# The modulation vector's products on VectorE inside the feed-forward stage, in a transformer block with a mixture of experts

## What is computed

```python
def first_block(...):
    h = h + fox_mixer(rms_norm(h, attn_norm), ...)
    gate, up = jnp.split(rms_norm(h, ffn_norm) @ ffn_w_in, 2, axis=-1)
    h = h + (jax.nn.silu(gate) * up) @ ffn_w_out
    return rms_norm(h, final_norm)
# the second block: c is (1, 1024), w_ada (1024, 6144)
mod = jax.nn.silu(c) @ w_ada + b_ada      # six vectors of 1024: shift, scale and gate, twice
```

## Time and profile before

| | |
|---|---|
| median of 3 runs | 2544.54 us |
| span of the profiled execution | 2545.1 us |
| TensorE busy | 2352.3 us, 92% |
| VectorE, ScalarE, GpSimd busy | 907.3, 738.5, 766.2 us |
| DMA | 597.33 MB, mean 235 GB/s |
| first feed-forward tile to end of the stage | 442.9 to about 811 us |

### The profile page before, as it was taken

The page is one execution under the profiler, slowest core; times in us unless marked ns, Lnnn a source line. Parts: engine busy times, 40 slices in busy tenths (PEclk is TensorE's granted clock), DMA queues, the critical chain, the costliest instruction groups (busy, mean ns, idle before and its releaser), DMA issues.

```text
span 2545.1 us, 26948 instructions
## 1 busy us (share of the span) xinstructions
PE 2352.3 (92%) x11046; PEld 1448.3 (57%) x11046; DVE 907.3 (36%) x1584; ACT 738.5 (29%) x1181; POOL 766.2 (30%) x488
## 2 busy tenths in 40 slices
PE   8999999999999999999999997998888888888885
PEld 5677557788888788787777883332322222322221
DVE  2634552100004799846775334211111111111113
ACT  3434562322223323348676222100100000001001
POOL 3233643454554344344233624110000100000000
PEclk9999999999999999999999998999999999999997
DMA  4344313532323333333335347999999999999994
GB/s 167 114 155 155 102 40 133 165 116 86 104 75 100 102 99 82 124 138 116 133 116 197 139 182 305 421 426 426 426 426 426 426 426 425 426 424 423 423 424 196
DMA packets 174202, 597.33 MB, mean 235 GB/s; under 512 B 18243, under 2 KB 97091, under 8 KB 148352
## 3 DMA queue, kind: packets, MB, share of 16 engines
q1 hardware_dynamic: 154992, 562.23, 56.8%
q10 hardware_dynamic: 8416, 23.92, 2.4%
q0 software_dynamic: 10672, 9.46, 1.1%
HBM read 591.02 MB, written 28.97 MB: 244 GB/s over the span
## 4 chain that ended last, share of the span: by engine, by line
PE 57%; DMA 24%; DVE 12%; ACT 4%; issue 2%; SPq 0%; POOL 0%; ACTq 0%; DVEq 0%; POOLq 0%
DMA arena<-in_w 14%; PE ps L785 11%; PE ps L787 10%; PE ps L786 10%; DMA ring<-in_w 9%; PE ps L1332 8%; DVE ps L2238 5%; PE ps L1330 3%; PE ps L1351 3%; DMA ring<-in_w_in 1%; PE ps L867 1%; ACT arena L1434 1%; PE ps L812 1%; PE ps L836 1%; PE ps L985 1%
## 5 line engine op out<-in xcount | busy, mean ns | idle before, releaser
L2684 POOL TENSOR_TENSOR ring_r<-ring,ring_r 128x1024 fp32r<-128x1024 f32 x220 | 511.6, 2332 | 687.3 <-ACT ring_r L1423 687.2
L785 PE MATMUL ps<-r,ring_r 128*128 128x512 f32 (+1 forms) x1536 | 611.9, 398 | 1.4 <-DVE arena L2226 1.2
L787 PE MATMUL ps<-r,ring_r 128*128 128x512 f32 (+1 forms) x1536 | 599.6, 390 | 0.0
L786 PE MATMUL ps<-r,ring_r 128*128 128x512 f32 (+1 forms) x1536 | 599.2, 390 | 0.0
L1434 ACT ACTIVATE arena<-ps 128x512 f32<-128x512 f32 (+4 forms) x274 | 183.2, 686 | 1145.5 <-PE ps L1332 854.1
L1332 PE MATMUL ps<-arena 128*64 128x512 f32 x672 | 325.5, 641 | 62.5 <-DMA arena<-in_w 62.1
L1330 PE MATMUL ps<-arena 128*64 128x512 f32 x688 | 345.6, 651 | 3.1 <-issue 3.0
L785 PEld LDWEIGHTS ps<-r,ring_r 128*128 128x128 f32 (+1 forms) x1536 | 287.6, 187 | 78.2 <-issue 14.6
L786 PEld LDWEIGHTS ps<-r,ring_r 128*128 128x128 f32 (+1 forms) x1536 | 287.8, 187 | 64.2 <-issue 4.3
L787 PEld LDWEIGHTS ps<-r,ring_r 128*128 128x128 f32 (+1 forms) x1536 | 287.4, 187 | 63.2
L1423 ACT ACTIVATE ring_r<-ring 128x1024 fp32r<-128x1024 f32 x220 | 222.9, 1015 | 322.2 <-PE ps L787 217.5
(11 more groups left out here) (357 smaller groups left out, 2466.4 us busy)
## 6 DMA issues: line engine op xcount, KB each, us to landing
arena<-in_w SPq DMA_DIRECT2D x106, 2048.0 KB, 39.1
ring<-in_w SPq DMA_DIRECT2D x86, 2048.0 KB, 37.5
ring<-in_w_ada SPq DMA_DIRECT2D x12, 2048.0 KB
ring<-in_ffn_w_in SPq DMA_DIRECT2D x22, 1024.0 KB
ring<-in_w_in SPq DMA_DIRECT2D x40, 512.0 KB
ring<-in_w_in SPq DMA_DIRECT2D x8, 2048.0 KB
ring<-in_fox_w_in SPq DMA_DIRECT2D x7, 2048.0 KB
arena<-acs_d SPq DMA_DIRECT2D x16, 512.0 KB, 3.5
```

Of the source, the lines that this page charges most:

```text
L785: e.matmul(out, wh[:, k, :], X.hi[:, k0 + k, :], start=first and k == 0, stop=False)
L786: e.matmul(out, wh[:, k, :], X.lo[:, k0 + k, :], start=False, stop=False)
L787: m = e.matmul(out, wl[:, k, :], X.hi[:, k0 + k, :], start=False, stop=last and k == nk - 1)
L2684: e.tensor_tensor(GL[t], grans[t][1], GH[t].bitcast(F32), ALU.subtract).then_inc(sem["gr_lo"], 1)
```

## The change

All twelve modulation tiles are made inside the feed-forward stage. VectorE multiplies and accumulates the eight blocks of a tile in two accumulators `AD` and adds them into `ADS`, which raises the semaphore `adv`; TensorE only sums `ADS` over the partitions, by `ones`. TensorE's products, ScalarE's copies and their places in the PSUM bank table are gone. The loads stand between the weight loads of the feed-forward stage, tile 0 to 5 with the pairs of tiles of the first half, 6 to 9 with the four blocks of the first down projection, 10 and 11 with the first two pairs of the second half. `order` exchanges every modulation load but the first with the load ahead of it. The slot of a modulation load is released by `adv`. The first rows of c go to the other slot, and their places in SyncE's list are renumbered.

```diff
+def ada_after(nt):
+    return (nt // 2 + 4 * (nt > 11),) if nt % 2 == 1 and 0 < nt < 16 else ()
+def ada_between(half, nt):
+    return (6 + nt // 2,) if half == 0 and nt % 2 == 1 else ()
 ...
     for k0, n in HALVES:
         for nt in range(k0, k0 + n, 2):
             two(a["ffn_w_in"], 128 * nt, FH + 128 * nt)
-            if nt < 8:
-                ada(8 + nt // 2)
+            for i in ada_after(nt + 1):
+                ada(i)
         for c in range(4):
 ...
+            for i in ada_between(k0 // 12, 2 * c + 1):
+                ada(i)
 ...
-        NCK0 = cols(RG[:, 0:1824], 2)
+        NCK0 = cols(RG[:, WC:WC + 1824], 2)
+        AD, ADS = [A[:, 26752 + 512 * i:27264 + 512 * i] for i in range(2)], A[:, 27776:28288]
 ...
-            return [(ps("ada", n).full, ps("ada", n).n + 1)]
+            return [(sem["adv"], n + 1)]
 ...
-            def ada(n):
 ...
-                    m = e.matmul(u.ap[32 * g:32 * g + 32], SC[:, k:k + 1].broadcast_to([128, 32]), aw[:, k, :], start=k < 4, stop=k >= 4)
+            def ada_columns(n):
+                u = ps("adb", n)
+                w.wait_ge(sem["adv"], n + 1)
                 w.wait_ge(u.free, u.n)
+                for j in range(4):
+                    m = e.matmul(u.ap[:, j:j + 1], ADS[:, j * 128:(j + 1) * 128], ones[:, 0:1], start=True, stop=True)
                 m.then_inc(u.full, 1)
 ...
                         whole("hu", nt, X=XF)
-                    if nt in (1, 3, 5):
-                        ada(9 + nt // 2)
+                    for n in ada_after(nt):
+                        ada_columns(n)
 ...
                             tile(u.ap, XH[half], u, k0=r, first=r == 0, last=r == 8)
+                        for n in ada_between(half, 2 * c + j):
+                            ada_columns(n)
 ...
+            def ada(n):
+                i, aw = ada_load[n]
+                w.wait_ge(sem["sc"], 1)
+                w.wait_ge(loads[i].slot, loads[i].value)
+                for k in range(8):
+                    acc = AD[k % 2]
+                    if k < 2:
+                        e.tensor_scalar(acc, aw[:, k, :], SC[:, k:k + 1], None, ALU.mult).then_inc(d.next(), 1)
+                    else:
+                        two_back()
+                        e.scalar_tensor_tensor(acc, aw[:, k, :], SC[:, k:k + 1], acc, ALU.mult, ALU.add).then_inc(d.next(), 1)
+                last()
+                e.tensor_tensor(ADS, AD[0], AD[1], ALU.add).then_inc(sem["adv"], 1)
 ...
                     e.tensor_tensor(x, x, u.ap, ALU.mult).then_inc(u.free, 1)
-                    if nt in (2, 4, 6):
-                        mod(8 + nt // 2)
+                    for n in (9,) if nt == 12 else ada_after(nt - 1):
+                        mod(n)
+                    for n in ada_after(nt + 1):
+                        ada(n)
 ...
                     e.tensor_tensor(hT[:, nt, NM:L], hT[:, nt, NM:L], u.ap, ALU.add).then_inc(u.free, 1)
+                    for n in (5,) if (half, nt) == (0, 0) else ada_between(half, nt - 1):
+                        mod(n)
+                    for n in ada_between(half, nt + 1):
+                        ada(n)
 ...
             order = list(range(len(loads)))
             for n, (i, _) in ada_load.items():
-                if n in (5, 6) or n >= 8:
+                if n > 0:
                     order[i - 1], order[i] = i, i - 1
```

More of the change, by code:

```diff
@@ L59 @@
         "nsq", "nrm", "lp_d", "lp_a", "cscan", "nckm", "qk", "sdone", "pmax", "pexp", "prec", "pnorm", "pv", "o_hi", "o_lo",
-        "fn", "fn_hi", "hid_hi", "hid_lo", "x2", "n1", "n1_hi", "uzero", "cv", "xbc", "bc", "alog", "acs",
+        "fn", "fn_hi", "adv", "hid_hi", "hid_lo", "x2", "n1", "n1_hi", "uzero", "cv", "xbc", "bc", "alog", "acs",
         "tk_d", "tk2", "cvc", "cvn", "cv_s", "cv_hi", "xs", "cb", "mrel", "mexp", "mm", "xd", "yg", "yl",
@@ L146, in bank_table @@
     t = ps.take
[L148 to L151, removed]
     def norm(stage, j, skip=()):
@@ L171, in bank_table @@
         t("ks", c)
-        ada(c, True)
     t("f", 0)
@@ L217, in bank_table @@
             t("hg", nt)
-            if nt in (2, 4, 6):
-                t("adb", 8 + nt // 2)
             t("hu", nt)
-            if nt in (1, 3, 5):
-                ada(9 + nt // 2)
+            for n in ada_after(nt):
+                t("adb", n)
         for nt in range(8):
             t("fo", half, nt)
+            for n in ada_between(half, nt):
+                t("adb", n)
     t("fin")
@@ L857, in spread @@
                 e.matmul(u.ap, ones, RST[:, :T], start=True, stop=True).then_inc(u.full, 1)
-            def ada(n):
[L860 to L863, removed]
+            def ada_columns(n):
+                u = ps("adb", n)
+                w.wait_ge(sem["adv"], n + 1)
                 w.wait_ge(u.free, u.n)
-                for k in range(8):
-                    g = k % 4
-                    m = e.matmul(u.ap[32 * g:32 * g + 32], SC[:, k:k + 1].broadcast_to([128, 32]), aw[:, k, :], start=k < 4, stop=k >= 4)
+                for j in range(4):
+                    m = e.matmul(u.ap[:, j:j + 1], ADS[:, j * 128:(j + 1) * 128], ones[:, 0:1], start=True, stop=True)
                 m.then_inc(u.full, 1)
[L870 to L876, removed]
             def meta(u, ld, raw):
@@ L1056, in pe @@
                         whole("hg", nt, X=XF)
-                        if nt in (2, 4, 6):
-                            ada_columns(8 + nt // 2)
                         whole("hu", nt, X=XF)
-                    if nt in (1, 3, 5):
-                        ada(9 + nt // 2)
+                    for n in ada_after(nt):
+                        ada_columns(n)
                 for c in range(4):
@@ L1973, in head_norm, with two_back @@
                 e.scalar_tensor_tensor(x, x, gain, RST[:, :n], ALU.mult, ALU.mult).then_inc(sem["nrm"], 1)
+            def two_back():
+                w.wait_ge(d.sem, d.n - 1)
+            def ada(n):
[11 more added lines that the diff above has]
+                e.tensor_tensor(ADS, AD[0], AD[1], ALU.add).then_inc(sem["adv"], 1)
             def mod(n):
@@ L2047, in dve @@
                 e.tensor_copy(kT[:, 4 * c:4 * c + 4, 0:NM], cols(u.ap[:, 0:64], 4)).then_inc(u.free, 1)
-                mod(c)
             for i in range(2):
@@ L2065, in dve @@
                 e.tensor_copy(vm[:, c * 512:(c + 1) * 512], u.ap[0:16]).then_inc(u.free, 1)
-                mod(2 + c)
             for nt in range(8):
-                if nt == 4:
-                    mod(4)
                 head_norm("q", nt)
-            mod(5)
             for nt in range(2):
                 head_norm("g", nt)
-            mod(6)
             w.wait_ge(sem["nrm"], 16)
@@ L2112, in dve @@
                 e.tensor_tensor(hT[:, nt, NM:L], hT[:, nt, NM:L], u.ap, ALU.add).then_inc(u.free, 1)
-                if nt in (4, 6):
-                    mod(7 + nt // 6)
                 if nt >= 3:
@@ L2862, in sp @@
                         w.wait_ge(s, value)
-                if i == 16:
+                if i == 9:
                     w.wait_ge(sem["c_d"], 16)
@@ L2872, in sp @@
                     e.dma_start(dst, src).then_inc(ld.slot, 16)
-                if i == 9:
+                if i == 5:
                     w.wait_ge(sem["cscan"], 1)
                     e.dma_start(a["c_d"], cT).then_inc(sem["c_d"], 16)
-                if i == 16:
+                if i == 9:
                     for p in range(2, 8):
```

52 lines of the change are left out of this document (removed).

## The result

The changed kernel takes 2688.3 us (median of four runs, 2687.07 to 2695.58) against 2544.17 us for the kernel before on the same chip: 1.0565 times as long, 95% interval 1.055 to 1.058. On another chip the ratio was 1.0575 (1.0556 to 1.0593). The profiled execution, one of the two quickest of the four, spans 2685.3 us, 140.2 us more than that of before; its mean granted clock is 0.937.

The account below looks back on a forecast made before the run. TensorE was taken to bound the kernel, busy for 92% of 2545.1 us. From 2544.5 us, -28.3 + 1.6 + 159.9 + 27, less 0.84, gave +159.4 and 2704 us, with 2668 to 2742 for 8 in 10.

Parts of the forecast that it names:

- the signs that it named: Feed-forward stage: TensorE idle some 13 us at eleven places, SyncE waiting for VectorE's last addition, clock near 0.5 behind stalls.
- What leaves TensorE: Ahead of the feed-forward stage: removed products and their sums shorten the time by 28.3 us.
- VectorE's modulation tile: Feed-forward stage: two multiplications, six multiply-adds and one addition on VectorE take 5.7 us a tile.
- The chain of a pair: From an even tile's gate to the next pair's ready weights: 36.7 us against TensorE's own pace of 22.6.
- The eleven stalls: Feed-forward stage: TensorE waits for late weights before seven tile pairs and four down-projection blocks, +159.9 us.
- 1.6: Feed-forward stage: twelve column sums replace three products and three sums on TensorE, +1.6 us.
- GpSimd beside VectorE: Modulation tiles in stalled cycles: VectorE meets no GpSimd split and keeps its clean 5.7 us, so nothing is added.
- its faster rival at 2518: Feed-forward stage: the weight load is in time anyway and only TensorE's work counts, 2518 us; chance 0.08.
- The clock: Behind each of eleven stalls: TensorE restarts at a low clock, 2.5 us each, +27 us, ends 0 and 37.
- the clock holds: Rival, feed-forward stage: the same stalls without the slow restart of TensorE's clock, 2677 us; chance 0.12.
- the port's lock (2730): Rival, feed-forward stage: GpSimd's splits block VectorE's chain each time, 2.4 us more per stall, 2730 us; chance 0.08.

Follow-up runs that it names:

- e6: Changed kernel with 30 short unused TensorE matmul calls (32 in the down projection) filling each of the eleven waits; ratio to the kernel before 1.0512.
- e3: Changed kernel with each modulation load bringing one row block of eight (256 KB for 2 MB); TensorE's waits for the split 88.9 us, no total time given.
- e1: Changed kernel without the exchange of loads, so each weight load goes ahead of the modulation load; ratio to the kernel before 0.9959, median of twelve executions 2559.04 us.
- e10: The changed kernel run again unaltered, on another chip; ratio to the kernel before 1.0575.
- e4: Changed kernel with 20 short unused TensorE matmul calls (about 10 us) in each of the eleven waits; ratio to the kernel before 1.0579.

## Why the prediction was right, and where its sizes were off

The forecast was 2704 us with 2668 to 2742, and 2688.3 came. The mechanism is the forecast's, and the signs that it named are there: eleven waits, at the gates of 2 to 14 and the four blocks of the first down projection; SyncE waiting for the last addition; the weight load right behind the modulation load; the slow clock behind each stall. Attention begins 20 us sooner (one of its first products at 244.05 for 264.17), where 23 were forecast.

- **What leaves TensorE**, -28.3: the first gate came 25.7 us sooner. Thirteen profiles with the same front part (the table) put it between 415.94 and 419.09, 24 to 27 us sooner. About 2 us of the shortfall are a wait of TensorE for ScalarE in the norms of v, 3.8 us for 1.7 in the kernel before. Of the first four products the last reads 4.0 us in the trace of before, not 3.6 (155.83 to 159.85), so the shortfall is 0.4 us larger than the two sizes tell.
- **VectorE's modulation tile**, 5.7: from the start of its first product (465.77) to the end of its last addition (471.34) 5.6.
- **The chain of a pair**, 36.7 without the clock: 35.0 in e6, where the clock held (35.9 less the 0.9 of the fillers). By steps, from the gate at 452.46: product at 11.3 (11.4), product to issue 6.3 (6.7), issue to weights 13.9 (14.6), hand-over 3.5 (4.0). The 6.3 us for the modulation load took its 2.10 MB as 2.0, at 317 GB/s it would be 6.6; yet e3 gave back only 4.7 us a stall for seven eighths of it, 5.4 for the whole.
- **The eleven stalls**, +159.9: this was the term furthest off. Of e6's 405.8 us 260.0 + 1.6 would be work without a stall, so 144.2 for the stalls at full clock, 1.4 us a stall less than predicted. It is spread over all of them: in e6, less what the fillers added, the cycle before a pair is 35.0 to 36.0 us (36.7 predicted), before the first block 33.7 (35.2), before the other three 30.9 to 31.8 (32.4), before tile 12 32.2 (33.9).
- **GpSimd beside VectorE**, 0: right, by the line with 740/743/750 ns. It was right because of the stall. Once the stall is gone, the collision is the next limit (e1), and the prediction didn't say so: its faster rival at 2518 met it, with executions from 2519 to 2565.
- **The clock**, +27: 18.9 in the changed kernel's profile, up to 22.0 by e10's. The prediction took 2.5 us a stall from rows of a restart behind short waits; measured are 1.7 to 2.0. That the slow work lies in the chain was right: TensorE is busy for 22 us more in the stretch (283.7 for 260.0 and 1.6), and 19.8 of them delay the product or addition that the chain waits for.

Summed up: -25.7 for -28.3, 1.6, 144.2 for 159.9, 18.9 for 27 and 1.1 behind the stage make the 140 us of the two profiles. The hit on the range wasn't made by errors that cancel: both large terms were taken too high, and the range had room for it. Of the rivals, "the clock holds" would have been 2677 and nearer to the time than the sum was, but its mechanism isn't there; the port's lock (2730) isn't either.

## What to carry to other kernels

When loads are issued in one order from one queue, a load that waits for a late engine is paid for by the load behind it; ask of every moved load what it waits for and which one stands next. Here putting the weights first took away the loss of 5.65%, though eight of the twelve executions stayed 0.6 to 1.1% above the kernel before, and moving the late work to where a cycle has room made it a small gain of 0.6 to 0.75%. An engine's idle time isn't room if another engine takes turns with it: with the stall removed, VectorE's chain of 5.6 us became one of up to 13.0 beside GpSimd's splits (e1, 696.35 to 709.35).

## What the runs showed of the hardware that I had not expected

- A pause of 3.5 us behind fillers at full clock cost as much as one of 10.6 to 14.9 us. In e4 the low clock lasted for 5 us of work behind the gate (0.50 in 492 to 497) and delayed the product by 2.8 us against e6; over all eleven gates the delays are 21.7 us, in the changed kernel 19.8 and in e10 24.1. Fillers that don't reach the gate saved nothing. Those that reached it held 1.00, but a filler too many delays the gate itself (7.5 us in e6).
- SyncE needed 4.13 us to issue the two weight DMAs right behind a modulation load of 2 MB, 1.06 behind one of 256 KB (e3) and 0.99 in the earlier trace rows. In these rows issuing took longer right behind the large load. Whether this or the engines' time sets the 14.9 us wasn't separated.
- A plain multiplication of VectorE with one tensor input waits for GpSimd's split just as a multiply-add does: 2668 ns at most for a median of 481.
